# Inverse levels of a chunked delta-rule scan: two chains of four heads, or four chains of two heads

## What is computed

```
a_mat = where(strict, (k * beta) @ k.T * decay, 0)         # per chunk and head
t_mat = inverse(eye + a_mat)                               # unit lower triangular
u     = t_mat @ (v * beta);   w = t_mat @ (k * beta * exp(g))
step:   v_new = u - w @ s;    o = q_dec @ s + qk @ v_new
        s     = s * exp(g_last) + k_dec.T @ v_new
```

## Time and profile before

| what | value |
|---|---|
| median of 3 runs | 3934.64 us (3934.12 to 3937.18) |
| the profiled execution | 3921.36 us |
| its span on the core | 3919.7 us, mean granted clock 0.894 |
| PE, share of the span | 79% |
| DVE, ACT, POOL | 31%, 17%, 10% |
| the scan's ten steps | from 706 us to 1141 us |

### The profile page before, as it was taken

The page is one execution under the profiler, slowest core; times in us unless marked ns, Lnnn a source line. Parts: engine busy times, 40 slices in busy tenths (PEclk is TensorE's granted clock), DMA queues, the critical chain, the costliest instruction groups (busy, mean ns, idle before and its releaser), DMA issues. The chain is left out here.

```text
span 3919.7 us, 53131 instructions
## 1 busy us (share of the span) xinstructions
PE 3082.5 (79%) x18254; PEld 1626.4 (41%) x18255; DVE 1220.7 (31%) x2185; ACT 669.2 (17%) x1490; POOL 409.9 (10%) x405
## 2 busy tenths in 40 slices
PE   4999998688877945999998467767879739969892
PEld 1454454687752342333333133335554513323330
DVE  3322322566663142111110341135551241101114
ACT  2211211111120020000000121136660100000002
POOL 0000000123211100000000212111111000000002
PEclk9999998889988957999999778889999759989996
DMA  5411110322234354778988320031102349987884
GB/s 194 135 34 54 41 29 25 110 69 83 69 125 157 119 206 180 323 303 352 403 312 343 134 100 32 28 109 59 40 20 97 119 172 388 386 345 285 346 333 155
DMA packets 152964, 667.96 MB, mean 170 GB/s; under 512 B 26144, under 2 KB 62144, under 8 KB 122080
## 3 DMA queue, kind: packets, MB, share of 16 engines
q1 hardware_dynamic: 123712, 540.57, 35.8%
q0 software_dynamic: 19504, 72.03, 4.9%
q10 hardware_dynamic: 9584, 53.19, 3.3%
HBM read 596.36 MB, written 69.39 MB: 170 GB/s over the span
## 5 line engine op out<-in xcount | busy, mean ns | idle before, releaser
L1609 PE MATMUL bank<-w,xT 128*64 x3392 | 752.5, 601 | 52.9 <-DMA w<-in_moe_w 43.0
L535 PE MATMUL bank<-aT,w 128*128 128x512 f32 (+1 forms) x1344 | 498.0, 533 | 8.0 <-DVE short L703 5.9
L1609 PEld LDWEIGHTS bank<-w,xT 128*64 128x64 f32 x3392 | 243.9, 139 | 522.0 <-issue 516.2
L1629 PE MATMUL bank<-w,hT 128*64 (+1 forms) x1696 | 380.8, 601 | 41.7 <-issue 41.5
L535 PEld LDWEIGHTS bank<-aT,w 128*128 128x128 f32 x1344 | 264.5, 198 | 237.4 <-issue 222.0
L1701 DVE TENSOR_TENSOR h<-h,bank 128x512 f32<-128x512 f32 x53 | 36.4, 688 | 784.1 <-PE bank L1609 784.1
L1629 PEld LDWEIGHTS bank<-w,hT 128*64 128x64 f32 x1696 | 123.8, 138 | 297.1 <-issue 294.9
L1899 PE MATMUL bank<-at_w_in,aT 128*128 128x512 f32 x416 | 191.3, 622 | 3.0 <-PEq L116 3.0
L2088 PE MATMUL bank<-eye,probs 128*128 128x128 f32 x640 | 102.2, 292 | 42.8 <-ACT probsT L2151 42.5
L1585 PE MATMUL bank<-eye,x 128*128 128x128 f32 x440 | 65.5, 295 | 83.3 <-DMA x<-moe_x,idx_block 58.3
L1558 POOL DMA_INDIRECT x<-moe_x,idx_block x55 | 53.4, 971 | 705.2 <-PE bank L1585 703.4
(11 more groups left out here) (324 smaller groups left out, 4140.1 us busy)
## 6 DMA issues: line engine op xcount, KB each, us to landing
w<-in_moe_w SPq DMA_DIRECT2D x180, 2048.0 KB, 14.4
ada_w<-in_ada_w SPq DMA_DIRECT2D x48, 1024.0 KB, 8.0
moe_y<-y ACTq DMA_DIRECT2D x53, 512.0 KB, 11.5
w<-in_moe_w ACTq DMA_DIRECT2D x12, 2048.0 KB, 13.8
w<-in_ab_w_in SPq DMA_DIRECT2D x28, 512.0 KB, 3.9
moe_x<-w SPq DMA_DIRECT2D x18, 512.0 KB, 2.6
moe_y<-zero POOLq DMA_DIRECT2D x1, 8192.0 KB, 26.2
at_w_in<-in_at_w_in SPq DMA_DIRECT2D x3, 2048.0 KB, 17.0
```

Source lines behind the costliest of these rows:

```text
L535: mm = pe.matmul(k.bank[3 * s + n][:, 0:width], w[j][:, c, :], aT[:, c, at:at + width], start=(c == 0), stop=(c == KC - 1))
L1609: mm = pe.matmul(k.bank[UP[half]][u * UNIT:(u + 1) * UNIT, :], xT[:, c, u * UNIT:(u + 1) * UNIT], w13[:, r if u else ds(buf[0], 1), half, ...
L1629: mm = pe.matmul(k.bank[Y[half]][u * UNIT:(u + 1) * UNIT, :], hT[:, c, u * UNIT:(u + 1) * UNIT], w2[:, r if u else ds(buf[0], 1), at:at + ...
```

## The change

The four heads of a direction are cut into two pairs, q = 0 and 1. A level is now four chains (q, d), each of half the size, and P, Pm, U and X are issued in the order (0,0), (0,1), (1,0), (1,1). The semaphores p_ready, u_ready, x_ready and pm_ready exist per direction and pair. P goes to bank 1 for pair 0 and bank 0 for pair 1, U to bank 2 and bank 3. The last merge is split in the same way, ACT's negated copies into two of 64x128 a direction. `ks` (bank 0) waits for the copies of the last merge of both pairs. X's start value is still made by one pair of instructions per direction; after it a semaphore instruction of DVE stands for the second pair. The matmuls are the same in number and shape.

The core of the diff:

```
-    both_new = [flat[d][2][:, 0:2 * NH * SUB]...(x=2, h=NH) for d in R2]
-    sub = [[flat[d][n][:, 0:NH * SUB]... for n in range(4)] for d in R2]
+    HQ = NH // 2
+    P_BANK, U_BANK = (1, 0), (2, 3)
+    both_new = [[flat[d][U_BANK[q]][:, 0:2 * HQ * SUB]...(x=2, h=HQ) for q in R2] for d in R2]
+    sub_p = [[flat[d][P_BANK[q]][:, 0:HQ * SUB]... for q in R2] for d in R2]
+    sub_u = [[flat[d][U_BANK[q]][:, 0:HQ * SUB]... for q in R2] for d in R2]
...
 # DVE
-                        X[d][:]..., ALU.subtract).then_inc(x_ready[d], 1)
+                        X[d][:]..., ALU.subtract).then_inc(x_ready[d][0], 1)
+                dve.sem_inc(x_ready[d][1], 1)
             for n in range(IN_SUB):
+                for q in R2:
+                    for d in R2:
+                        dve.wait_ge(p_ready[d][q], primed(s * MERGES + n + 1))
+                        nc.vector.tensor_tensor(Pm[d][:, pair(q), :], sub_p[d][q], ..., ALU.mult).then_inc(pm_ready[d][q], 1)
+                for q in R2:
+                    for d in R2:
+                        dve.wait_ge(u_ready[d][q], primed(s * MERGES + n + 1))
+                        dve.wait_ge(x_ready[d][q], primed(s * XS + n + 1))
+                        nc.vector.tensor_tensor(X[d][:, :, pair(q), :], X[d][:, :, pair(q), :], both_new[d][q],
+                                                ALU.subtract).then_inc(x_ready[d][q], 1)
...
 # PE
             for n in range(IN_SUB):
+                for q in R2:
+                    for d in R2:
+                        pe.wait_ge(x_ready[d][q], primed(s * XS + n + 1))
+                        pe.sem_inc(tiles_begun, 1)
+                        for h in range(HQ):
+                            for b in range(0, P, SUB):
+                                mm = pe.matmul(sub_p[d][q][at(b), h, :], ...)
+                        mm.then_inc(p_ready[d][q], 1)
+                for q in R2:
+                    for d in R2:
+                        pe.wait_ge(pm_ready[d][q], primed(s * MERGES + n + 1))
+                        if n == 0:
+                            pe.wait_ge(kq_ready[d], primed(s + 1))
...
+                        mm.then_inc(u_ready[d][q], 1)
...
             for d in R2:
                 pe.wait_ge(s_ready[d], primed(s))
+                for q in R2:
+                    pe.wait_ge(pm_ready[d][q], primed(s * MERGES + MERGES))
                 heads(bank[d][0], KT[d][u], S[d]).then_inc(ks_ready[d], 1)
...
 # ACT
             for d in R2:
+                for q in R2:
+                    act.wait_ge(u_ready[d][q], primed(s * MERGES + MERGES))
+                    turned = nc.scalar.activation(TT[d][at(lo), pair(q), at(hi)], sub_u[d][q][at(lo)], ACT.Copy, scale=-1.0)
+                turned.then_inc(tf_ready[d], 1)
```

More of the change, by code:

```diff
@@ L777, in TT_sub, with pair @@
         return X[d][:, 1 - d]
+    def pair(q):
+        return slice(HQ * q, HQ * q + HQ)
     def at(b):
@@ L898, in body @@
             for d in R2:
-                act.wait_ge(x_ready[d], primed(s * XS + XS))
+                for q in R2:
+                    act.wait_ge(x_ready[d][q], primed(s * XS + XS))
                 act.wait_ge(vn_ready[d], primed(s))
@@ L968, in body @@
[L968 to L975, removed]
+                for q in R2:
+                    for d in R2:
+                        dve.wait_ge(p_ready[d][q], primed(s * MERGES + n + 1))
+                        nc.vector.tensor_tensor(Pm[d][:, pair(q), :], sub_p[d][q],
+                                                merge[:, d, n + 1, :].unsqueeze(1).to_broadcast([P, HQ, SUB]),
+                                                ALU.mult).then_inc(pm_ready[d][q], 1)
@@ L1037, in body @@
+            for q in R2:
                 for d in R2:
-                    if n == 0:
-                        pe.wait_ge(vd_ready[d], primed(s))
-                        pe.wait_ge(vn_copied[d], primed(s))
-                    pe.wait_ge(x_ready[d], primed(s * XS + n + 1))
+                    lo, hi = low_high(d)
+                    pe.wait_ge(x_ready[d][q], primed(s * XS + XS))
                     pe.sem_inc(tiles_begun, 1)
-                    for h in range(NH):
-                        for b in range(0, P, SUB):
-                            mm = pe.matmul(sub[d][1][at(b), h, :], AT[d][at(b), h, at(b)], T_sub(d)[at(b), h, :],
-                                           start=True, stop=True)
@@ L1047, in body @@
-                    mm.then_inc(p_ready[d], 1)
+                    for h in range(HQ * q, HQ * q + HQ):
+                        mm = pe.matmul(sub_p[d][q][at(hi), h - HQ * q, :], AT[d][at(lo), h, at(hi)], T_sub(d)[at(lo), h, :],
+                                       start=True, stop=True)
+                    mm.then_inc(p_ready[d][q], 1)
+            for q in R2:
                 for d in R2:
-                    pe.wait_ge(pm_ready[d], primed(s * MERGES + n + 1))
-                    if n == 0:
-                        pe.wait_ge(kq_ready[d], primed(s + 1))
+                    lo, hi = low_high(d)
+                    pe.wait_ge(pm_ready[d][q], primed(s * MERGES + MERGES))
```

64 lines of the change are left out of this document (29 added, 35 removed).

## The result

The kernel after the change took 3949.06 us (median of 8 runs, 3945.48 to 3957.82) against 3934.23 us (8 runs, 3924.84 to 3937.18): a ratio of 1.0045, 95% interval 1.0033 to 1.0057. The forecast was 3914 us, and it had the sign wrong. The profiled executions took 3951.34 us after (span 3949.6) and 3921.36 us before.

The account below looks back on a forecast made before the run. The loop of P, U and X in each scan level was taken as the bound, neither PE nor DVE full. Ten steps of 2.43 us, less 3 us for low clock, gave 21 us off 3934.6: 3914 us, range 3905 to 3925.

Parts of the forecast that it names:

- So a level takes 2.91 us instead of 3.42: Scan levels: four half-size chains save 0.51 us a level, 2.55 us over the five levels of a step.
- the rival on that: Levels: small DVE instructions don't overlap, 4 us lost in all, 3918 us; chance 0.22 together with dearer handovers.
- 0.01 us a group: Scan step: price on PE of each of 24 added groups with wait and increment, 0.24 us a step.
- The rivals of 0.03 and 0.05 us a group and of a start anew: Price per group in a level: 0.03 us, 3920 us (0.22 with DVE rival); 0.05, 3930 (0.08); anew 0.15, 3976 (0.04).
- rule of a serial tail for increments: Added increments at matmul ends: some 26 ns each, estimated 6 us in all, leaving 17 us or so gained, not 21.
- The 0.47 us lost in the first level: First level of each step: the last chain starts two half P later than P1 did, 0.47 us lost.
- The 0.59 us gained in the last merge: Last merge of each step: halved P, U and copy shorten the chain up to `ks` by 0.59 us.
- 2.67 - 0.24 = 2.43 us: Scan step at full clock: 2.67 us from levels and their ends, less 0.24 us for added groups.
- the 3 us that I took off: First levels at low clock: 0.35 us less gain in each of nine steps, 3 us in all.
- What is added: Scan step: 24 more PE groups cost 0.24 us; the added ACT, DVE and `ks` work costs nothing on the path.
- the gain is eaten: Rival in the levels: at 0.05 us a group only 5 us is gained, 3930 us; chance 0.08.
- slower 0.04: Rival in the levels: PE starts each of eight groups anew, 4.02 us a level, 41 us lost, 3976 us; chance 0.04.

Follow-up runs that it names:

- after_unroll_lean: Changed kernel, scan loop written out, unawaited increments at PE's group heads removed, 182 skipped instructions behind the scan: 3904.43 us, ratio 0.9923.
- before_shift: Kernel before the change with 104 satisfied waits of PE at the start of the gating stage behind the scan: 3954.22 us, ratio 1.0060.
- again: The changed kernel run once more, nothing altered: 3950.13 us, ratio 1.0057.
- before_pad8: Kernel before the change with eight satisfied waits ahead of P1 in each level: 3940.71 us, ratio 1.0026.

## Why the prediction was wrong

**The level.** "So a level takes 2.91 us instead of 3.42": right, 2.92 us in eleven of the 40 inner periods of the kernel after (these run from the end of one level's last X to that of the next). Taken at their undisturbed length they would be 116.8 us instead of 136.8, the 20 us that were forecast. They were 136.9 us, and before 141.2 us: 20.1 us lay on top, against 4.4 us before. Of the 20.1 us some 15 us are stops that stand in these levels; part of the rest is the clock behind them, 1.2 GHz for 5 us of these levels. In after_unroll_lean they were 116.5 us, with 2.9 us on top.

**DVE.** The instruction of 128 elements takes 287 ns (forecast 0.29 us) and that of 256 takes 421 ns; four follow one another in 1.01 us, so they overlap, and the rival on that falls.

**The price of a handover.** I took 0.01 us a group, and an undisturbed level shows still less: it stands 0.10 us over PE's 2.82 us, and most of that is one break ahead of the last P (its first load starts 109 ns behind the one before, where loads within a group follow after some 30 ns), where the schedule had a wait of 0.09 us for X. Without separate waits the level stands 0.02 us over PE's time, so part of that break belongs to the separate instruction; either way the eight groups together cost 0.1 us at most. The rivals of 0.03 and 0.05 us a group and of a start anew fall with it. The Trainium skill's rule of a serial tail for increments ("TensorE: Matmul & The Clock Gate", section "The cost: per-tile semaphore tail") has some 26 ns each where every matmul increments. Here a group of four or eight matmuls increments once, at its end, and eight groups stand 0.02 us in all over PE's time, so this kernel pays nothing like it.

**The ends of the levels.** The 0.47 us lost in the first level was right: against the 0.51 us of any level it left a gain of 0.04 us, and from the start value to the first X the best steps took 3.53 us before and 3.50 us after. The 0.59 us gained in the last merge was too large: from the last X to `ks` it was 1.97 us and is 1.77 us, 0.20 us. Four inner levels by 0.50 us, 0.03 us in the first and 0.20 us in the merge make 2.2 us a step at full clock, where the sum had 2.67 - 0.24 = 2.43 us.

**The clock.** The ten first levels together took 47.1 us before and 51.3 us after, which looks like the 3 us that I took off. But this moves between executions as much as between the kernels: 50.4 us in before_shift, 49.0 us in again. The runs don't show that the change itself costs clock in the first levels. What no term had is the clock lost behind a halt, as at 907.00 us.

**The step that failed** is one that isn't in the sum. "What is added" gave 24 groups a step the price of their time on PE, and nothing for what they do to the delivery of PE's own code. The trace of before showed the symptom: PE stopped for 6.3 us in three places of L1014 with no semaphore, at the turns of the loop, and once in the middle of a P, in the second level of another step:

```profile
1027.07 0.59 PE L1045 MATMUL bank<-T_TT_sub,AT 64*64 64x64 f32 x13 [0.25 <-DVE T_TT_sub L971]
1028.97 0.33 PE L1045 MATMUL bank<-T_TT_sub,AT 64*64 64x64 f32 x3 [1.31 <-issue]
```

I read the engine's waits for other engines only. The first consequence is in the scan: each level has eight separate waits instead of four, stops grow by 10 to 31 us at an equal place of the loop (11 to 22 us by the issue rows), and the gain is gone. The second is behind it: 104 instructions more in PE's program move all later code within its 16 KB pieces, 11 to 21 us by the medians. "What the scan loses or gains goes into the end one to one; nothing outside overlaps it" was true of the loads and false of the code.

The rivals were all priced inside the level, so none held this outcome; "the gain is eaten", the nearest, had a wrong mechanism. I gave slower 0.04 on one mechanism that the schedule excluded.

**What stays open.** That the stops end with the arrival of code is shown; why separate waits make its transfer begin late isn't. It may be that PE's sequencer, held at one, asks for the next piece only when it moves on; the trace has the start of each packet, but not what set it off. That the removal did it, and not a lucky place of the written-out code, rests on one kernel; but the places tried moved the scan by 15 us, and this one by 34 us, and in no other placement of the changed kernel with all its matmuls and its separate waits were the issue rows under 20.8 us. The increments and the separate instructions were removed together, and only with the loop written out, as the wait then is for a constant. The kernel before with the same two edits wasn't run, so how much of the 27 us gained is the four chains and how much the rest isn't measured; its undisturbed level is 3.42 us against 2.84 us. Nor do the runs explain why half the matmuls freed the kernel after of its stops (8.4 us, issue rows 7.2 us) and not the kernel before (20.4 us, issue rows 15.9 us), or how the place of the code acts on the stages behind the scan.

## What to carry to other kernels

Before pricing a change on a densely packed TensorE, look for "issue" among its waits, in the middle of groups of equal matmuls, and set the packets of the instruction queue beside them: if PE goes on soon after a packet's end, it is code that arrives late, and a shorter schedule can turn all of its gain into it. Then try to let waits ride on the matmuls and to drop increments that nobody waits for; here that was worth 36 us, in the one form tried, with the loop written out. And before explaining a difference of half a per cent, compare stages that were not edited: if they moved, put the later code back where it was with instructions that are never run, and measure again.

## What the runs showed of the hardware

- Instructions that never run are worth 11 us of 3940: 146 of them behind a branch brought the changed kernel from 3949 to 3938 us; 104 satisfied waits took the kernel before from 3930 to 3954 us, 7 us of it their own time.
- The time behind the scan depends on the place of PE's code with a period of 256 instructions: 2767 to 2774 us at 0 (eleven kernels), 2792 to 2794 us at 104 (three), in profiled executions, with the same instructions executed.
- PE stood still without a semaphore until 1.3 to 1.8 us after the end of a 16 KB packet of q8 in 22 of 23 cases of the kernel after; a packet took 0.9 to 1.2 us.
- The place of the loop within its 16 KB moves a scan of 440 us by up to 15 us. Each of its three turns back costs a stop of 1.6 to 2.2 us on PE.
- A satisfied wait as an instruction of its own takes PE 0.025 us between dense groups (before_pad8) and 0.07 to 0.08 us in a row of 104 to 152.
- Sixteen loads of 128x128 fp32 took 1.86 us at full clock where 32 of 64x64, which cover the blocks that matter, took 1.15 us, and a level grew from 2.92 to 3.94 us: filling up a block-diagonal weight to save instructions cost a third more time.
